# 32 columns of each token block gathered ahead; the full gather in two groups of tiles around the first pair's down products

## What is computed

```python
t = h.reshape(-1, d)
g_sel = jnp.argmax(g_logits, axis=-1)                       # 4 groups of 8 experts
top_v, top_i = lax.top_k(e_logits, TOPK_EXPERT)             # 2 experts of the chosen group
w_top = jax.nn.softmax(top_v, axis=-1) * p_group[:, None]
comb = jnp.sum(jax.nn.one_hot(eid, N_EXPERTS) * w_top[..., None], axis=1)
hg = jnp.einsum('nd,edf->nef', t, w_gate)
hu = jnp.einsum('nd,edf->nef', t, w_up)
a = jax.nn.silu(hg) * hu * comb[:, :, None]
y = jnp.einsum('nef,efd->nd', a, w_down)
```

## Time and profile before

| what | us |
|---|---|
| median of 3 runs | 766.99 (766.43 to 768.08) |
| the profiled execution | 765.26 |
| its span, first to last instruction | 762.7 |
| PE busy | 730.6 (96% of the span) |
| DVE busy | 354.0 |
| ACT busy | 188.0 |

### The profile page before, as it was taken

How to read it: one execution, slowest core, us unless ns; L and a number is a source line. 1 busy time by engine, 2 the same in 40 slices (tenths; PEclk the granted TensorE clock), 3 DMA queues, 4 the chain that set the end, 5 groups by cost and what they waited for, 6 DMA issues and landing times.

```text
span 762.7 us, 9761 instructions
## 1 busy us (share of the span) xinstructions
PE 730.6 (96%) x3883; PEld 485.9 (64%) x3883; DVE 354.0 (46%) x798; ACT 188.0 (25%) x412; POOL 58.8 (8%) x69
## 2 busy tenths in 40 slices
PE   6999999998889999999989999999999999999996
PEld 4677778786524434343334886788888888885442
DVE  2125666785721212121121876364276656567445
ACT  5014323533511111111011338131321111111002
POOL 3033660040000000000001000000000000000000
PEclk9999999999999999999999999999999999999999
DMA  9998956956999999999999963123454645443401
GB/s 339 339 339 249 396 192 222 354 205 261 351 377 415 416 414 416 418 413 415 419 409 368 371 227 111 46 66 111 151 181 135 197 146 185 157 175 111 165 28 58
DMA packets 78250, 197.27 MB, mean 259 GB/s; under 512 B 3343, under 2 KB 38520, under 8 KB 72312
## 3 DMA queue, kind: packets, MB, share of 16 engines
q1 hardware_dynamic: 77248, 195.37, 68.6%
q10 hardware_dynamic: 664, 0.80, 0.4%
q0 software_dynamic: 288, 0.41, 0.3%
HBM read 195.33 MB, written 1.05 MB: 257 GB/s over the span
## 4 chain that ended last, share of the span: by engine, by line
PE 75%; SPq 10%; DMA 7%; DVE 5%; ACT 1%; issue 1%; POOL 1%; DVEq 0%; ACTq 0%
PE ps L1502 18%; PE ps L1218 9%; PE ps L777 9%; PE ps L1563 9%; PE ps L1294 5%; PE ps L903 4%; PE ps L1127 4%; SPq L572 4%; PE ps L914 2%; DMA arena<-in_w_up 2%; DMA ring<-in_w_ada 2%; SPq L578 2%; PE ps L1089 2%; PE ps L1099 2%; DMA ring<-in_w_in 2%; PE ps L1303 2%
## 5 line engine op out<-in xcount | busy, mean ns | idle before, releaser
L1218 PE MATMUL ps<-ring,arena 128*64 128x512 f32 x352 | 77.6, 593 | 3.1 <-DMA ring<-in_w_up 2.5
L903 PE MATMUL ps<-hs,ring 128*128 128x256 f32 (+1 forms) x288 | 66.2, 384 | 1.0 <-DMA ring<-in_w_in 1.0
L903 PEld LDWEIGHTS ps<-hs,ring 128*128 128x128 f32 (+1 forms) x288 | 52.7, 187 | 12.7 <-issue 3.8
L1218 PEld LDWEIGHTS ps<-ring,arena 128*64 128x64 f32 x352 | 26.3, 137 | 52.5 <-issue 52.5
L2848 DVE SCALAR_TENSOR_TENSOR arena<-arena,own_rows,ps 128x256 f32<-128x256 f32 x16 | 7.7, 480 | 106.8 <-ACT arena L1884 106.8
L777 PE MATMUL ps<-hs,ring 128*128 128x256 f32 x240 | 53.3, 381 | 0.3 <-PE ps L777 0.3
L777 PEld LDWEIGHTS ps<-hs,ring 128*128 128x128 f32 x240 | 45.2, 190 | 7.1 <-issue 0.9
L1502 PE MATMUL ps<-ring,hs 128*128 128x256 f32 x176 | 41.7, 380 | 0.9 <-DVE xT L2727 0.9
L1502 PE MATMUL ps<-ring,mixT 128*128 128x256 f32 x176 | 41.7, 380 | 0.0
L1502 PE MATMUL ps<-arena,mixT 128*128 128x256 f32 x176 | 41.6, 379 | 0.0
L1294 PE MATMUL ps<-ring,arena 128*64 128x512 f32 x176 | 40.2, 598 | 1.0 <-issue 0.5
(11 more groups left out here) (483 smaller groups left out, 1215.5 us busy)
## 6 DMA issues: line engine op xcount, KB each, us to landing
ring<-in_w_down SPq DMA_DIRECT2D x23, 1024.0 KB, 18.1
ring<-in_w_gate_up SPq DMA_DIRECT2D x22, 1024.0 KB, 7.2
ring<-in_w_gate SPq DMA_DIRECT2D x18, 1024.0 KB, 17.1
ring<-in_w_up SPq DMA_DIRECT2D x18, 1024.0 KB, 17.9
ring<-in_w_ada SPq DMA_DIRECT2D x5, 3072.0 KB, 12.9
ring<-in_w_down SPq DMA_DIRECT2D x5, 2048.0 KB, 8.1
ring<-in_w_in SPq DMA_DIRECT2D x9, 1024.0 KB, 17.1
ring<-in_w_ada SPq DMA_DIRECT2D x16, 512.0 KB, 9.3
```

Of the source, the lines that this page charges most:

```text
L903: last = pe.matmul(o[0:n, 0:L], lhsT=w[:, k, lo:lo + n], rhs=h[:, k, :], start=k == 0, stop=k == KT - 1)
L1218: last = pe.matmul(ps[WIN * h:WIN * (h + 1), 0, :].rearrange("p (g n) -> p g n", g=2), lhsT=xw[:, u, k, :], rhs=expert_gate_up(2 * n + h, ...
```

## The change

The first 32 columns of each block of pick are made first (four short VectorE steps), and gather_first forms the 64 columns that team 0 needs, for all 8 tiles, in two halves of four tiles in PSUM banks 3 and 1. VectorE adds the shift and writes them to xw as team 0's window. The full gather stays, on all columns, and goes behind team 0's gate/up products: tiles 0 and 1, the turn of team 0's result, tile 2, team 0's down products, tiles 3 to 7, in banks 2, 3, 4, 5, 6, 7, 3, 4. ScalarE and VectorE take its tiles between team 0's steps; team 1's window is copied behind the last tile. SP's loads of the near quarters of expert 5 move behind both halves of experts 6 and 7 and wait for the whole gather (gather_done 10). In the other path (too_many set) the full gather follows the small one.

```diff
--- before.py
+++ after.py
@@ -110,7 +110,8 @@
 SQUARED = {2: 0, 4: 2, 6: 4}
 SCALED = {3: 0, 2: KT, 4: 2 * KT, 5: 3 * KT}
 GROUP_COLS = 8
-FIRST_TILES = 6
+FIRST_TILES = 4
+GATHER_BANKS = (2, 3, 4, 5, 6, 7, 3, 4)
 ROUTE_COLS = GROUP_COLS + EXPERTS
 ORDER = ([("ada0", 0, 3, 0), ("ada0", 3, 2, 1), ("ada0", 7, 1, 2), ("in", 0, 1, 3), ("ada", 0, 1, 0), ("in", 1, 1, 1), ("in", 2, 2, 2), ("ada", 1, 1, 0), ("in", 3, 2, 3),
           ("ada", 2, 1, 1), ("ada", 3, 1, 0), ("in", 4, 1, 2), ("ada", 4, 1, 1), ("ada", 5, 1, 2),
@@ -623,10 +624,6 @@
             sp.wait_ge(ada_rows_done, 9)
             load_gate_up(2)
             load_down(2)
-            sp.wait_ge(gather_done, 1)
-            load_quarter(5, 0, 0)
-            sp.wait_ge(gather_done, 1 + KT)
-            load_quarter(5, 1, 0)
             def load_early_halves(k_half):
 
                 at = k_half * D
@@ -641,6 +638,9 @@
                 sp.wait_ge(gate_up_used, team - HOMES // 2 + 2)
                 if team == HOMES // 2:
                     load_early_halves(1)
+                    sp.wait_ge(gather_done, 2 + KT)
+                    load_quarter(5, 0, 0)
+                    load_quarter(5, 1, 0)
                 elif team == TEAMS - 1:
                     for k_half in range(2):
                         load_last_halves(k_half)
@@ -1191,20 +1191,36 @@
             pe.wait_ge(ada_pool_ready, 6)
             quarters(6, ones[:, 0:Q], w[:, PE_K, :], last=True).then_inc(ada_rows_done, 1)
 
-            def gather():
+            def gather_first():
 
                 pe.wait_ge(htr_taken_a, 4)
-                for b in range(BLK):
-                    pe.wait_ge(pick_ready, b + 1)
-                    for j in range(KT):
-                        if b == 0 and j == 6:
-                            pe.wait_ge(row_taken, 8)
-                        last = pe.matmul(ps[:, j, b * L:(b + 1) * L], lhsT=tok[:, b, j * P:(j + 1) * P], rhs=pick[:, b, :],
-                                         start=b == 0, stop=b == BLK - 1, skip_group_check=True)
-                        if b == BLK - 1:
-                            last.then_inc(gather_done, 1)
-                    if b == 0:
-                        last.then_inc(gather_done, 1)
+                for half, bank in enumerate((3, 1)):
+                    for b in range(BLK):
+                        if half == 0:
+                            pe.wait_ge(pick_ready, b + 1)
+                        for i in range(FIRST_TILES):
+                            j = half * FIRST_TILES + i
+                            last = pe.matmul(ps[:, bank, i * WIN + b * SUB:i * WIN + (b + 1) * SUB],
+                                             lhsT=tok[:, b, j * P:(j + 1) * P], rhs=pick[:, b, 0:SUB],
+                                             start=b == 0 and i == 0, stop=b == BLK - 1 and i == FIRST_TILES - 1,
+                                             skip_group_check=True)
+                    last.then_inc(gather_done, 1)
+
+            def gather(tiles):
+
+                for j in tiles:
+                    if j == 0:
+                        pe.wait_ge(pick_ready, 2 * BLK)
+                        pe.wait_ge(first_windows, 2)
+                    if GATHER_BANKS[j] == 6:
+                        pe.wait_ge(row_taken, 8)
+                    if j >= 6:
+                        before = GATHER_BANKS.index(GATHER_BANKS[j])
+                        pe.wait_ge(gather_taken_v if before % 2 else gather_taken_a, before // 2 + 1)
+                    for b in range(BLK):
+                        last = pe.matmul(ps[:, GATHER_BANKS[j], b * L:(b + 1) * L], lhsT=tok[:, b, j * P:(j + 1) * P],
+                                         rhs=pick[:, b, :], start=b == 0, stop=b == BLK - 1, skip_group_check=True)
+                    last.then_inc(gather_done, 1)
 
 
             def gate_up(n, u, first=False, late=False):
@@ -1614,14 +1630,18 @@
             pe.wait_ge(windows_ready, 2)
             pe.wait_ge(pad_ready, 6)
             too_many = pe.value_load(flag_i[0:1, 0:1], min_val=0, max_val=1)
+            gather_first()
             with pe.If(too_many < 1):
-                gather()
                 weights_there(0)
                 gate_up(0, 0, first=True).then_inc(gu_done, 1)
+                gather((0, 1))
                 pe.wait_ge(act_ready, 2)
                 turn_act(0)
+                gather((2,))
                 pe.wait_ge(turn_taken, 1)
+                pe.wait_ge(gather_taken_a, 1)
                 down_joined(0)
+                gather(range(3, KT))
                 for n in range(1, TEAMS):
                     next_team(n)
                 pe.wait_ge(put_taken, TEAMS // 2)
...
@@ -1868,25 +1888,29 @@
             act.wait_ge(windows_ready, 2)
             too_many = act.value_load(flag_i[0:1, 0:1], min_val=0, max_val=1)
 
-            def take_gathered():
-
-                for j in range(0, KT, 2):
-                    act.wait_ge(gather_done, j + 2)
-                    act.activation(xsT[:, j, 0:PAIRS], ps[:, j, :], ACT.Identity, bias=shift_q[:, j:j + 1]
+            def take_gathered(tiles):
+
+                for j in tiles:
+                    act.wait_ge(gather_done, j + 3)
+                    act.activation(xsT[:, j, 0:PAIRS], ps[:, GATHER_BANKS[j], :], ACT.Identity, bias=shift_q[:, j:j + 1]
                                    ).then_inc(gather_taken_a, 1)
 
-            def team_act(n, u, fast):
+            def team_act(n, u, fast, first=False):
 
                 act.wait_ge(gu_done, n + 1)
                 if fast:
                     act.sem_inc(gate_up_used, 1)
                 act.wait_ge(act_ready, n + 1)
                 act.activation(act_g, ps[:, 0, 0:FE], ACT.Silu).then_inc(silu_done, 1)
+                if first:
+                    take_gathered((0,))
                 act.wait_ge(turn_done, n + 1)
...
                 act.activation(act_turned[:, u, :], ps[:, 1, 0:FE], ACT.Copy).then_inc(turn_taken, 1)
+                if first:
+                    take_gathered((2,))
                 m = n // 2
                 if u:
                     act.wait_ge(put_done, m + 1)
@@ -1895,6 +1919,8 @@
                     last.then_inc(put_taken, 1)
                 act.wait_ge(chunk_used, 2 * n + 2)
                 act.activation((y_low if u else y_high)[m % 2][WIN:P], ps[WIN:P, 2, :], ACT.Copy).then_inc(y_taken, 1)
+                if first:
+                    take_gathered((4, 6))
 
             def second_block():
 
@@ -2046,12 +2072,11 @@
                 row_out(0)
 
             with act.If(too_many < 1):
-                take_gathered()
                 for n in range(TEAMS):
-                    team_act(n, n % 2, True)
+                    team_act(n, n % 2, True, n == 0)
                 second_block()
...
@@ -2396,13 +2421,25 @@
                              AX.X, ALU.add).then_inc(dve_step, 1)
             own()
             for b in range(BLK):
-                if b:
-                    ve.wait_ge(pick_ready, b)
-                half, found = col_no[:, b * L:(b + 1) * L], tmp_cols
+                ve.tensor_scalar(tmp_cols[:, b * SUB:(b + 1) * SUB], col_no[:, b * L:b * L + SUB], cols[:, 1, b:b + 1], None,
+                                 ALU.is_equal).then_inc(dve_step, 1)
+            for b in range(BLK):
+                own()
+                ve.scalar_tensor_tensor(pick[:, b, 0:SUB], col_no[:, b * L:b * L + SUB], cols[:, 0, b:b + 1],
+                                        tmp_cols[:, b * SUB:(b + 1) * SUB], ALU.is_equal, ALU.add).then_inc(pick_ready, 1)
+            for b in range(BLK):
+                ve.wait_ge(pick_ready, BLK + b)
+                half, found = col_no[:, b * L + SUB:(b + 1) * L], tmp_cols[:, SUB:L]
                 ve.tensor_scalar(found, half, cols[:, 1, b:b + 1], None, ALU.is_equal).then_inc(dve_step, 1)
                 own()
-                ve.scalar_tensor_tensor(pick[:, b, :], half, cols[:, 0, b:b + 1], found, ALU.is_equal, ALU.add
+                ve.scalar_tensor_tensor(pick[:, b, SUB:L], half, cols[:, 0, b:b + 1], found, ALU.is_equal, ALU.add
                                         ).then_inc(pick_ready, 1)
+            for half, bank in enumerate((3, 1)):
+                tiles = slice(half * FIRST_TILES, (half + 1) * FIRST_TILES)
+                ve.wait_ge(gather_done, half + 1)
+                ve.tensor_tensor(xw[:, 0, tiles, :], ps[:, bank, 0:FIRST_TILES * WIN].rearrange("p (k n) -> p k n", n=WIN),
+                                 shift_q[:, tiles].unsqueeze(2).broadcast_to([P, FIRST_TILES, WIN]), ALU.add
+                                 ).then_inc(first_windows, 1)
 
             starts_4d = starts_f.rearrange("p (b q h) -> p b q h", b=BLK, h=2)
             for w in range(WINDOWS):
@@ -2460,18 +2497,14 @@
             def take_gathered(tiles):
 
                 for j in tiles:
-                    ve.wait_ge(gather_done, j + 2)
-                    ve.tensor_scalar(xsT[:, j, 0:PAIRS], ps[:, j, :], shift_q[:, j:j + 1], None, ALU.add
```

(22 more changed lines are left out.)

## The result

The changed kernel takes **769.98 us** (median of 7 runs, 768.75 to 771.72), the kernel before 766.43 us (median of 7 beside it, 764.74 to 768.08): ratio **1.0051, 95% interval [1.0038, 1.0064]**. It is slower by about 3.9 us by the ratio. The profiled execution of after took 769.75 us (span 767.9), that of before 765.26 us (span 762.7). TensorE's granted clock falls to 1.2 GHz for 3.4 us at varying places of some executions, so that one profile beside another can be 1 to 2 us off; the profile of before has no such stretch in the expert stage. Times are compared by the runs, places by the profiles.

The account below looks back on a forecast made before the run. The prediction took the weight stream, full for good from about 226 us, as the bound: 3.0 us later on the profiled 765.26 us gives 768.3, plus 1.7 to the median gives 770.0 us, range 767.3 to 772.0 us.

Parts of the forecast that it names:

- The bound: Expert stage: its end follows when the weight stream is full for good; team 4's first byte was at 226.3 us before.
- The small gather: TensorE ahead of team 0: 32 instructions at 0.112 us, 3.6 us, to 199.85 us; halves evicted at 198.8 and 200.6 us.
- Gate/up of team 0: TensorE's first products: start at 200.0 us, 4.4 us earlier than before, and end at 206.9 us.
- VectorE's chain: VectorE ahead of team 0's first silu: ready only at 209.4 us, leaving 2.4 of the 4.4 us won.
- SP's queue: SP's loads: expert 5's quarters wait until 219.5 us; engines stand still from 215.7 or 217.4 to 220.5 us.
- The stream's shift: Team 4's first byte: 2.6 to 3.5 us later than 226.3 us, taken as 3.0 us.
- the fourth rival: New order around team 1: branch, takes in turn or slow restart make it another 2 us later, 772.0 us and up; 0.08.
- The sum: Whole kernel: 3.0 us on the profiled 765.26 us gives 768.3; with 1.7 to the median, 770.0 us.
- The stream never runs dry: First rival, load engines: whole gather done in time, 2.7 us lost from 208 to 219 us come back; 764.3 us; 0.07.
- The small gather is cheap: Second rival, TensorE's small gather: 0.041 us spacing, 1.3 us in all; team 4 1.55 us earlier, 768.5 us; 0.13.
- TensorE sets the end: Third rival, expert stage: engines make up the gap, TensorE's waits swallow its 3.65 us; 766.0 to 767 us; 0.10.
- More waits: Fourth rival, new order: branch, takes in turn, slow restart; team 1 another 2 us later, 772.0 us and up; 0.08.

Follow-up runs that it names:

- the delay at team 1: Kernel before with five idle TensorE products more at the start of team 1: 769.71 us, ratio 1.0037.
- the downs first: Changed kernel with the down weights of experts 6 and 7 ahead of expert 5's quarters and their wait on SP: 769.96 us, ratio 1.0041 of before.
- the pair of delays: Kernel before with the same five idle TensorE products, once at team 6 (765.61 us, ratio 0.9985), once at team 1 (769.71 us, 1.0037).
- the pieces: Kernel before with early halves of experts 6 and 7 loaded in three pieces: 766.44 us; with team 4's weights in halves too: 766.39 us.
- the shorter chain: Changed kernel with VectorE's register load moved from ahead of the ranks to behind team 1's rows: 769.39 us, ratio 1.0042 of before.
- 128 columns: Changed kernel with 128 instead of 32 columns per block in the small gather: 771.06 us; with VectorE's register load moved later too: 769.98 us.
- the order on SP: Kernel before with only expert 5's quarters moved behind the early halves on SP: 767.90 us, ratio 1.0026.

## Why the prediction was right, and where its steps were not

The forecast of 770.0 us came with the mechanism that carried it: the first bytes of team 4, held back by team 1's products behind five late tiles, shift a stream that never gains anything back. Point by point:

- **The bound** holds. The same delay is free at team 6 and costs 2.8 us at team 1; the last wait for weights is still there, and longer.
- **The small gather** took 0.111 us for each instruction (0.112 said), and the two halves were evicted at 198.56 and 200.35 us (198.8 and 200.6 said). The Trainium skill, "TensorE: Matmul & The Clock Gate", section "Back-to-back issue gap", has about 25 ns for an isolated matmul of so few columns; this run of weight loads and products does not come near it, with 0.111 us for 32 columns. That 128 moving columns have the same spacing fits weight loads that set it.
- **Gate/up of team 0** started as said (199.82 for 200.0) and ended 1.6 us later than said, at 208.5 us: this step failed. The clock was at 1.2 GHz from 200.3 us for 3.4 us, directly behind the 32 short products; no step of mine had it. It cost almost nothing at the end, because it lay in the 1.75 us of idleness that I had put ahead of the turn. In the kernel with the downs ahead of the quarters the clock did not fall: gate/up took 7.09 us, TensorE idled 1.45 us ahead of the turn, and team 1 started at 220.79 us, only 0.25 us earlier. What it did move were the early halves, issued at 205.21 and 208.69 us for 203.7 and 207.2 said (203.30 and 206.78 there).
- **VectorE's chain** was the late one, with the silu at 209.32 us (209.4 said), the turn at 210.36 (210.35), down 0 at 211.54 (211.45), team 1 at 221.04 (220.8) and team 4's issue at 228.21 us (227.9).
- **SP's queue**: the quarters were issued at 219.74 us (219.5 said), and the engines stood still ahead of them. That they are covered holds: team 2, which needs expert 5, starts at 233.63 us without a wait.
- **The stream's shift** is the term that was mis-sized: 3.0 us taken, 4.4 in the bytes and 5.4 at the landing of expert 29 (395.40 us for some 393 said). The first byte of team 4 came at 229.57 us where 226.12 was the time before, 3.45 us later (2.6 to 3.5 said, and of two bounds of which the later must rule I took the middle). Some 0.9 us more is a slow start that I had counted only for the quarters: the engines move 250 GB/s at 230 us, and the fourth rival's third item (a slow restart) is true to that extent. It shows in the others too: with the delay at team 1 the first byte is 3.0 us later and the lag about 3.5, with the downs first 2.8 and 3.3. The last 1.0 us, the late last step of expert 29's semaphore, stands in no step of mine, and its cause stays open.
- **The sum** came out at 770.0 all the same. I had 768.3 us for the profiled execution, which took 769.75, and added 1.7 for what before lay under its median; after, it lies 0.2 under. So 4.5 us between the two executions (769.75 less 765.26) are 3.5 between the medians, and 3.9 by the ratio, where the forecast had 3.0. That the forecast lies within 0.1 us of the median is chance; the mechanism gives 3 to 5 us.
- **The rivals.** *The stream never runs dry* falls with 8 and 53 GB/s at 219 to 221 us. *The small gather is cheap* falls with 0.111 us for each instruction. *TensorE sets the end* falls with the pair of delays. *More waits* has only the slow start.

Open: why the pieces gain nothing, why the last step of expert 29's semaphore falls behind, and what the quarters' place costs in the times.

## What to carry to other kernels

Where loads run at full rate for a long stretch, ask of a change not when the first engine starts, but when the queue of loads is full for good, and follow each wait that stands on that queue: here 4 us lost ahead of that moment cost 2.8 us at the end, and the same 4 us behind it were free. A head start for the first step buys nothing if the work it skipped is put in front of the step that releases the next loads. And the start of the first step is only worth what the slowest of the chains beside it (here VectorE's) lets through.

## What was not expected of the hardware

- Behind 32 products of 32 moving columns the granted clock fell to 0.5 (1.2 GHz) for 3.4 us, at 200.3 us, in the changed kernel's profile and at 199.5 us in that of the shorter chain, but not in that of the downs first, and behind 128 columns in neither of two profiles; that the width is the cause is not shown. In the kernel before and its variants it fell at 213.5 to 214.1 us, behind the 1.2 us in which TensorE waits ahead of the first turn, in three profiles of seven, and at 188.6 us in two others. In times: of the 35 runs of before beside the order on SP, 8 with a mean clock of 0.999 have a median of 765.37 us, 9 with 0.997 one of 766.83, 5 with 0.993 one of 769.82; one such stretch is 0.0022 of the mean.
- Loads that come into empty engines start slowly. In the changed kernel they move 274 GB/s from 222 to 226 us; with the delay at team 1 team 4's loads move 147 GB/s in the first microsecond and 393 in the second, against 414 in the long run. The same loads ran at 414 GB/s from 227 to 228 us before, where no pause stood ahead of them, so there it is the pause and not the form of the loads. Behind team 4's first byte this costs about 0.5 us on top of the pause itself, with the delay at team 1 and with the downs first. Why the slow stretch lasts one microsecond there and four with the quarters was not told apart.
